# Gate and up projections of a two-block transformer kernel: the seven-product scheme applied inside each block product in every second weight slot

## The reference, cut to what matters

```python
def swiglu_ffn(u, w_gate_up, w_down):          # u (1, 512, 1024)
    g, up = jnp.split(u @ w_gate_up, 2, axis=-1)   # w_gate_up (1024, 2 * 2816)
    return (jax.nn.silu(g) * up) @ w_down          # w_down (2816, 1024)
...
D_MODEL, SEQ, DEPTH = 1024, 512, 2
D_FF = 2816
```

## Time and profile before

| | |
|---|---|
| median of 3 runs | 2923.05 us (2922.53 to 2923.17) |
| span of the profiled execution | 2921.3 us, first to last instruction |
| PE busy | 2810.8 us, 96% of the span |
| PE weight loads busy | 1896.7 us, 65% |
| DVE, ACT, POOL busy | 1110.9, 663.0, 512.2 us |
| gate and up, slots 1 to 10, layer 1 and layer 2 | about 242 us each, from 1674 and from 2538 us |

### The profile page before, as it was taken

One profiled execution on the slowest core, in us unless ns is written; L12 is line 12 of the kernel. 1 busy time (PEld: TensorE's weight loads), 2 busy tenths in 40 slices (PEclk: granted clock), 3 DMA queues, 4 the chain that ended last, 5 costly groups with the idle time before them and its releaser, 6 DMA issues.

```text
span 2921.3 us, 32166 instructions
## 1 busy us (share of the span) xinstructions
PE 2810.8 (96%) x12444; PEld 1896.7 (65%) x12444; DVE 1110.9 (38%) x2252; ACT 663.0 (23%) x1512; POOL 512.2 (18%) x785
## 2 busy tenths in 40 slices
PE   8999999899999998999999999999999999999998
PEld 4565543355656432686565688888686575788887
DVE  4543311154433111445432333354446332333354
ACT  3333110033331100105422211101206412211100
POOL 3101111131111111113200022201114410122201
PEclk9999999999999999999999999999999999999999
DMA  3206799831067998420020222222220111122222
GB/s 135 75 29 252 292 425 423 363 127 56 30 259 305 424 425 359 175 87 30 30 87 29 87 87 87 72 80 94 87 87 30 49 67 47 69 87 87 72 90 84
DMA packets 106579, 422.13 MB, mean 145 GB/s; under 512 B 10096, under 2 KB 14320, under 8 KB 91440
## 3 DMA queue, kind: packets, MB, share of 16 engines
q1 hardware_dynamic: 93104, 387.01, 34.1%
q0 software_dynamic: 12736, 30.84, 2.8%
q10 hardware_dynamic: 576, 2.10, 0.2%
HBM read 408.63 MB, written 27.26 MB: 149 GB/s over the span
## 4 chain that ended last, share of the span: by engine, by line
PE 77%; issue 9%; DMA 7%; DVE 2%; ACT 2%; POOL 1%; POOLq 1%; DVEq 0%; SPq 0%; ACTq 0%
PE ps L2551 35%; PE ps L1773 6%; DMA ring_feat<-in_w 5%; PE ps L431 5%; PE ps L2792 4%; PE ps L2819 4%; PE ps L1112 3%; PE ps L1814 3%; PE ps L2693 2%; PE ps L2839 2%; PE ps L3153 2%; PE ps L1339 2%; PE ps L2283 1%; PE ps L2070 1%; PE ps L2265 1%
## 5 line engine op out<-in xcount | busy, mean ns | idle before, releaser
L431 PE MATMUL ps<-ring_feat 128*128 128x512 f32 (+2 forms) x704 | 274.9, 545 | 4.9 <-DMA ring_feat<-in_w_lat 2.8
L2551 PE MATMUL ps<-ring_feat 128*128 128x256 f32 x1216 | 277.0, 379 | 1.6 <-ACT big L287 1.6
L2551 PE MATMUL ps<-big 128*128 128x256 f32 x1200 | 268.1, 379 | 0.0
L2551 PEld LDWEIGHTS ps<-ring_feat 128*128 128x128 f32 x1216 | 230.9, 190 | 34.5 <-issue 3.3
L2551 PEld LDWEIGHTS ps<-big 128*128 128x128 f32 x1200 | 228.0, 190 | 31.0
L431 PEld LDWEIGHTS ps<-ring_feat 128*128 128x128 f32 x704 | 132.7, 191 | 130.6 <-issue 93.6
L2551 PE MATMUL ps<-tmp 128*128 128x256 f32 x576 | 128.6, 379 | 0.0
L2551 PE MATMUL ps<-ring_feat,tmp 128*128 128x256 f32 x544 | 126.6, 379 | 0.0
L2551 PEld LDWEIGHTS ps<-tmp 128*128 128x128 f32 x576 | 109.3, 190 | 14.8
L2792 PE MATMUL ps<-ring_feat 128*128 128x512 f32 x256 | 113.9, 596 | 5.0 <-ACT ring_feat L3052 2.7
L1112 PE MATMUL ps<-ring_feat 128*128 128x512 f32 x256 | 113.7, 595 | 0.0
(11 more groups left out here) (501 smaller groups left out, 4663.8 us busy)
## 6 DMA issues: line engine op xcount, KB each, us to landing
big<-in_w SPq DMA_DIRECT2D x36, 2048.0 KB, 20.8
ring_feat<-in_w SPq DMA_DIRECT2D x36, 2048.0 KB, 27.7
ring_feat<-in_w_gate_up SPq DMA_DIRECT2D x22, 2048.0 KB, 8.0
ring_feat<-in_w_mix_in SPq DMA_DIRECT2D x12, 2048.0 KB, 8.1
e_spare<-in_w SPq DMA_DIRECT2D x12, 1792.0 KB, 25.7
par<-in_w SPq DMA_DIRECT2D x12, 1536.0 KB, 23.6
ring_feat<-in_w_down SPq DMA_DIRECT2D x12, 1536.0 KB, 6.7
tmp<-in_w_mem_kv SPq DMA_DIRECT2D x6, 2048.0 KB, 25.2
```

Of the source, the lines that this page charges most:

```text
L431: yield T.matmul(bank, lhs(k), rhs(k), start=k == 0, stop=k == n - 1)
L2551: m = T.matmul(to, lhs[:, j, :], rhs[:, j, :], start=start and j == 0, stop=stop and j == chunks - 1)
```

## The change

In slots 1 to 10 the two chunks of a slot are joined. Each of the seven products is now taken over the whole slot (256 columns of each half), in one order for all slots: P1, P6, P7, P5, P2, P4, P3. The intermediate `corner` blocks C11, C12, C21, C22 are four rows in SBUF. Two kinds of slot alternate:

- *One-level slots* (1, 3, 5, 7, 9), called O below: each product is two block products as before (8 matmuls of 128x128 against 256 tokens). The SBUF and PSUM operations around them are now 128x512, half as many.
- *Two-level slots* (2, 4, 6, 8, 10), `TWO_LEVEL`, called E below: each of the seven products is itself done by the seven-product scheme. Its operands are cut once more into 2x2 (two chunks by 128 columns, two chunks by 128 tokens), so a product is 7 x 2 = 14 matmuls of 128x128 against **128** tokens, and its result is 7 x 128 = 896 columns over two banks. The inner recombination is linear, so it is not done per product: the seven inner parts are carried through the outer additions, which become 128x896, and are recombined once per corner at the end (`corners`, POOL, seven additions of 128x256 for two corners at once).

For an E slot the inner sums of seven left operands have to be made (`form_left`, six by DVE with four operations of 128x256 each, and `weight_sums` for a22 by POOL), and once per layer those of the seven right operands (`form_right` two by DVE, `token_sums` five by POOL). They are kept in spare places (`spare_piece`) and in the parts of the slot that are no longer needed. The outer weight sums have one set of buffers, `s_block`, in place of two, so they are overwritten as soon as PE has used them. PSUM spaces are four, of two banks each, used in turn (`product_space`): a product waits until the one four before it has been read. The last multiplications of slot 10 (`gate_end`) move behind the down projection's second set of sums, and the down projection waits for them at its slot 3, not at slot 1.

The core of the diff:

```diff
+        X11, X12, X21, X22 = [(slice(k, k + 2), slice(f, f + P)) for f in (0, P) for k in (0, 2)]
+        SLOTS_UP = range(1, FC // 2)
+        TWO_LEVEL = range(2, FC // 2, 2)
+        PRODUCTS = ("P1", "P6", "P7", "P5", "P2", "P4", "P3")
+        LEFT = dict(P1="a11", P6="s2", P7="s3", P5="s1", P2="a12", P4="a22", P3="s4")
+        RIGHT = dict(P1="b11", P6="t2", P7="t3", P5="t1", P2="b21", P4="t4", P3="b22")
+        SEVEN = 7 * P
+        s_block = {f"s{i + 1}": view(big, 4096 + i * 1024, KC // 2, 256) for i in range(4)}
+        corner = view(big, 8192, 4, SEVEN)
...
+            def product(p, n):
+                w, to = slot_w["pe", n][1], product_space(l, p, n)
+                x, tok = left_block(w, LEFT[p]), RIGHT[p]
+                if n not in TWO_LEVEL:
+                    for i in range(2):
+                        m = block_product(to[:, i * 256:(i + 1) * 256], x[:, :, i * P:(i + 1) * P], right_block(tok))
+                    return m
+                y11, y12, y21, y22 = right_parts(tok)
+                s1, s2, s3, s4 = left_sums(l, w, LEFT[p])
+                t1, t2, t3, t4 = right_sums(l, tok)
+                for q, (lhs, rhs) in enumerate(((part(x, X11), y11), (part(x, X12), y21), (s4, y22), (part(x, X22), t4),
+                                                (s1, t1), (s2, t2), (s3, t3))):
+                    m = block_product(to[:, q * P:(q + 1) * P], lhs, rhs, 2)
+                return m
...
+            for n in SLOTS_UP:
+                two = n in TWO_LEVEL
+                for p in PRODUCTS:
+                    op, tok = LEFT[p], RIGHT[p]
+                    if p == "P1":
+                        ring_n = slot_w["pe", n][0]
+                        pe.wait_ge(w_loaded[ring_n % 2], 16 * (ring_n // 2 + 1))
+                    if two and op == "a22":
+                        pe.wait_ge(*outer(l, op, n))
+                    elif two or op[0] == "s":
+                        pe.wait_ge(*formed(l, op, n))
+                    if p == "P4":
+                        pe.wait_ge(*formed(l, "s4", n))
+                    if n == TWO_LEVEL[0] and tok in TOKENS_AT:
+                        pe.wait_ge(*tokens(l, tok))
+                    space_free(p, n)
+                    product(p, n).then_inc(bank_full if p == "P4" else up_full, 1)
...
+        def up_act(act, l):
...
+            for n in SLOTS_UP:
+                if n > 1:
+                    act.wait_ge(*added(l, "low", n - 1))
+                copy("P1", C11, n)
+                if n > 1:
+                    silu(C12, n - 1)
+                copy("P7", C21, n)
+                if n > 1:
+                    act.wait_ge(*added(l, "high", n - 1))
+                copy("P5", C22, n)
+                silu(C11, n)
+            silu(C12, LAST_UP)
...
+        def form_left(dve, l, op, n):
...
+            w = slot_w["dve", n][1]
+            x = left_block(w, op)
+            dve.drain()
+            form_sums(dve, *[part(x, b) for b in (X11, X12, X21, X22)], left_sums(l, w, op)).then_inc(blocks_summed, 1)
...
+        def up_dve(dve, l):
...
+            for n in SLOTS_UP:
+                two_now, two_next = n in TWO_LEVEL, n + 1 in TWO_LEVEL
+                if n > 1:
+                    last_corner(n - 1)
+                form_slot(dve, l, n)[3]()
+                if n > 1:
+                    multiply(0, n - 1)
+                if two_now:
+                    form_left(dve, l, "s4", n)
+                if n > 1:
+                    multiply(1, n - 1)
+                if n == 1:
+                    form_right(dve, l, "b11")
+                    form_right(dve, l, "t2")
+                dve.wait_ge(*full(l, "P6", n))
+                dve.wait_ge(*copied(l, "p1", n))
+                dve.drain()
+                V.tensor_tensor(corner[:, C12, 0:width_of(n)], product_space(l, "P6", n), corner[:, C11, 0:width_of(n)],
+                                ALU.add).then_inc(hidden_ready, 1)
+                if n < LAST_UP:
+                    third, second, first, fourth = form_slot(dve, l, n + 1)
+                    third()
+                    second()
+                    if two_next:
+                        dve.wait_ge(*full(l, "P1", n))
+                        form_left(dve, l, "a11", n + 1)
+                        form_left(dve, l, "s2", n + 1)
+                        form_left(dve, l, "s3", n + 1)
+                    first()
+                    if two_next:
+                        form_left(dve, l, "s1", n + 1)
+                else:
+                    dve.wait_ge(*full(l, "P7", n))
+                    down_sums(dve, l, 0, slot_w["dve", n][0] + 1)
+                add("P2", C11, n).then_inc(hidden_ready, 1)
+                dve.wait_ge(*outer(l, "c22", n))
+                add("P4", C21, n).then_inc(hidden_ready, 1)
+                if two_next:
+                    form_left(dve, l, "a12", n + 1)
+            last_corner(LAST_UP)
...
+        def up_pool(pool, l, before_end):
...
+            def corners(half, n):
+                pool.wait_ge(*added(l, ("c21", "c12")[half], n))
+                q = [in_halves[:, half, :, i * P:(i + 1) * P] for i in range(7)]
...
+                def add(to, more):
+                    return G.tensor_tensor(out=q[to], in0=q[to], in1=q[more], op=ALU.add)
...
+                add(5, 0)
+                add(1, 0)
+                pool.drain()
+                add(6, 5)
+                pool.drain()
+                add(5, 4)
+                add(3, 6)
+                pool.drain()
+                add(2, 5)
+                add(4, 6).then_inc(outer_added, 1)
...
+            for n in SLOTS_UP:
+                if n - 1 in TWO_LEVEL:
+                    corners(1, n - 1)
+                c12, c21, c22 = (corner[:, c, 0:width_of(n)] for c in (C12, C21, C22))
+                pool.wait_ge(*added(l, "u2", n))
+                pool.wait_ge(*copied(l, "p7", n))
+                G.tensor_tensor(out=c21, in0=c21, in1=c12, op=ALU.add).then_inc(outer_added, 1)
+                if n == 1:
+                    token_sums("t4")
+                pool.drain()
+                pool.wait_ge(*copied(l, "p5", n))
+                G.tensor_tensor(out=c12, in0=c12, in1=c22, op=ALU.add).then_inc(outer_added, 1)
+                pool.drain()
+                G.tensor_tensor(out=c22, in0=c22, in1=c21, op=ALU.add).then_inc(outer_added, 1)
+                if n + 1 in TWO_LEVEL:
+                    weight_sums(n + 1)
+                if n == 1:
+                    pool.wait_ge(bank_full, before_end)
+                    token_sums("t1")
+                    token_sums("b22")
+                if n in TWO_LEVEL:
+                    corners(0, n)
```

More of the change, by code:

```diff
@@ new lines, in program, with part, spare_piece @@
+        corner = view(big, 8192, 4, SEVEN)
+        C11, C12, C21, C22 = range(4)
+        in_halves = corner.rearrange("p (r h) n -> p h r n", h=2)
+        def part(v, block):
+            return v[:, block[0], block[1]]
+        def spare_piece(l, i):
+            for buf, first, n in ((e_spare, 0, 14), (rows, 0, 6), (cst, P, 14), (par[l], PAR2["mix_post"][0], 8),
+                                  (par[l], PAR2["sub_g"][0], 1), (big, 11776, 2)):
+                if i < n:
+                    return view(buf, first + i * 256, 2, P)
+                i -= n
@@ new lines, in up_act, with copy, silu @@
+        def up_act(act, l):
+            up_slots("act", l)
+            def copy(p, to, n):
+                act.wait_ge(*full(l, p, n))
+                A.activation(corner[:, to, 0:width_of(n)], product_space(l, p, n), ACT.Copy).then_inc(silu_ready, 1)
+            def silu(c, n):
+                if n in TWO_LEVEL:
+                    act.wait_ge(*outer(l, ("low", "high")[c], n))
+                else:
+                    act.wait_ge(*added(l, ("c11", "c12")[c], n))
+                gate = results(c, n)
+                A.activation(gate, gate, ACT.Silu).then_inc(silu_ready, 1)
+            for n in SLOTS_UP:
[10 more added lines that the diff above has]
+            silu(C12, LAST_UP)
@@ new lines, in gate_up @@
+            n = take(name, "ring")
+            w = ring_slot(n, KC, 512)
+            if name == "pe":
+                eng.wait_ge(w_loaded[n % 2], 16 * (n // 2 + 1))
+                first, second, banks = slice(0, 2 * P), slice(2 * P, 4 * P), []
+                feat_ready(eng, 1)
+                for i in range(2):
+                    for o, reader in ((i * P, "act"), (256 + i * P, "dve")):
+                        banks.append((open_bank(eng, reader), o))
+                        up_at[l, i] = count[("pe", "bank")] - 1
+                        products(banks[-1][0], w, o, first)
+                    if i == 0:
+                        turn_x(name, eng, TT - 1)
+                feat_ready(eng, 3)
+                for bank, o in banks:
+                    products(bank, w, o, second).then_inc(bank_full, 1)
+                    take(name, "full")
```

(19 more changed lines are left out.)

349 lines of the change are left out of this document (208 added, 141 removed).

## The result

The changed kernel takes 2939.63 us (median of four, 2935.82 to 2940.6) against 2922.89 for the kernel before (median of four; the 2923.05 above is that of three): a ratio of 1.0052 [1.0037, 1.0066], slower by half a per cent. I had forecast 2900.4 us, in a range of 2893 to 2917. PE's own work shrank about as forecast, but PE then waited for longer than it had saved.

What follows compares the result with a forecast made beforehand. PE, busy 96% of 2921.3 us and without a gap in this stage, was taken as the bound. Shorter E slots (-23.5) and stalls (+0.8) gave -22.7, so 2898.6, plus 1.75 from span to median: 2900.4 us, range 2893 to 2917.

Steps and rivals of the forecast that it cites:

- What bounds the kernel before, and PE's saving: Slots 1 to 10: PE's records set the time; E slots fall from 24.1 to 21.8 us, saving 23.5 in all.
- Rival 1: E slots: the pace of short records does not last over 196 in a row; no gain, 2923 us, chance 0.08.
- Single durations: DVE, ACT and POOL operations taken singly: for 128x896, DVE 1.09 us, ACT 0.9, POOL 2.1; POOL 1.27 for 512.
- At the ratio of rows 10 (+0.31 in 0.69) they cost DVE 1.2 to 1.7: O slot: POOL's three 512-wide additions delay DVE by 1.2 to 1.7 us, scaled from one DVE sum stretched beside POOL.
- 0.8 us for stalls of all kinds: Each of 8 transitions from O to the next E: 0.1 us of PE stall, 0.8 us in the sum.
- if they take turns wholly, 3.8: Same three POOL additions, dear end: DVE and POOL exclude each other, costing DVE 3.8 us and missing the slack by 0.6.
- The slack of 3.2 becomes 1.5 to 2.0: C11 of O, before P6 of the next E: 3.2 us early, still 1.5 to 2.0 after DVE's delays beside POOL.
- the heavy half: DVE's work after an E slot's second multiplication, through sums and additions to O's C11: from 33.5 to 45.8 us.
- The end of slot 10: Down projection's first sums come before C11 as now, `rest` due only at its slot 3; no cost set.
- Rival 2: Corners: POOL's additions slow to 1.53 us, PE stands 8 us in each of 8 transitions; 2964 us, chance 0.12.
- POOL's 20 token operations (15 us) lie under slots 0 and 1: Start of each layer: POOL's token sums, 15 us, are hidden under slots 0 and 1, costing PE nothing.

Runs made afterwards that it cites:

- e5: Changed kernel with POOL's three outer additions of every joined slot on 8 columns, not 512 or 896 (values wrong): 2901.37 us, 0.991 of the kernel before.
- e4: Changed kernel with POOL's fourteen corner additions on 2 x 8 elements, not 2 x 128 (values wrong): 2907.9 us, 0.9939 of the kernel before.
- e9: Changed kernel with the high half's seven corner additions moved from POOL to DVE: 2909.53 us, 0.9942 of the kernel before.
- e11: Changed kernel with POOL's outer and corner additions replaced by fills that read nothing (values wrong): 2903.61 us, 0.9923 of the kernel before.
- e7: Changed kernel with only slots 2, 5 and 8 two-level: 2914.3 us, 0.9956 of the kernel before.

## Why the prediction was wrong, step by step

- **What bounds the kernel before, and PE's saving: right.** An E slot takes 21.95 us against my 21.8, ten save 22.0 us against 23.5, and the pace of 0.112 holds for a slot of 196 records. Rival 1 fell. e5, where PE never waits in the stage, shows it whole: 46.04 us a pair.
- **Single durations: right where nothing meets.** POOL's 512 took 1.27 (forecast 1.27, the middle of a range of 1.09 to 1.45, so with some luck), DVE's 896 1.09 (1.09), ACT's 0.92 (0.9).
- **"At the ratio of rows 10 (+0.31 in 0.69) they cost DVE 1.2 to 1.7": this step failed.** Rows 10 hold no ratio. POOL's row ahead of those shown, from the trace of before:

```profile
1911.02 0.64 POOL L3140 TENSOR_TENSOR cst<-cst,rows 128x256 f32<-128x256 f32 x1 [9.59 <-ACT rows L3112]
```

It ends at 1911.66, and DVE's stretched sum (1911.20, 1.00) ends 0.54 us later. The DVE sum waited for the end of POOL's operation. It came out at +0.31 only because POOL's operation had 0.46 us left when it began. The earlier trace rows hold the full wait: POOL's 1.53 began 0.19 us into DVE's sum of 1.23 and ended 0.49 after it. I had written the price of full turns beside the sum and left it out for rows 10. The sum had 0.8 us for stalls of all kinds; PE's waits and the slow records behind them came to 17.0 + 17.4 = 34.4. The changed kernel shows the same at the end of slot 10, against POOL's 896-wide additions; DVE, then POOL, in order of time:

```profile
1905.57 2.57 DVE L2526 TENSOR_TENSOR big<-tmp 128x512 f32<-128x512 f32 x1
1908.21 2.42 DVE L2528 TENSOR_TENSOR big<-big,tmp 128x512 f32<-128x512 f32 x1
1910.70 2.41 DVE L2530 TENSOR_TENSOR big<-tmp,big 128x512 f32<-128x512 f32 x1
```

```profile
1905.13 2.46 POOL L3450 TENSOR_TENSOR big<-big 128x896 f32<-128x896 f32 x1 [7.02 <-DVE big L3369]
1907.75 2.33 POOL L3455 TENSOR_TENSOR big<-big 128x896 f32<-128x896 f32 x1 [0.16 <-issue]
1910.24 2.32 POOL L3457 TENSOR_TENSOR big<-big 128x896 f32<-128x896 f32 x1 [0.16 <-issue]
```

POOL's ends are 1907.59, 1910.08 and 1912.56; DVE's are 1908.14, 1910.63 and 1913.11, each 0.55 later. Three sums of 0.69 take 7.4 us. The stretched 1024-wide sums above end 1.1 us after the POOL operation that they met (1785.28 + 2.13 = 1787.41 against 1784.15 + 2.17 = 1786.32), the 256-wide ones 0.28 after it. A longer POOL operation makes a longer wait, and the change made them 3.5 times as wide. So the kind of price at the dear end of my range, "if they take turns wholly, 3.8", was right. That its size agrees with the 3.9 us measured over the pass is partly luck: POOL's three 512-wide additions cost DVE 2.9, and the other 1.0 came from POOL's sums of a22, which I had priced for POOL alone.

- **"The slack of 3.2 becomes 1.5 to 2.0": the wrong question even at the right price.** I laid out one pair from PE's beginning and held each operation against its deadline, one contact at a time. But C11 is late by what the corners before it were late by, and those by the u2 before them. Closed, the ring without turns is some 41.4 us, about what my own durations add up to, under PE's 46.1: a slack of 4.7 for all of it. Turns take 3.9 in the heavy half and beside a22, 2.5 at the 896-wide outer additions, which I had priced as if alone, and 0.5 at the corners: 2.2 us too many in each pass, and every pass adds its own. A slack that I put at 1.5 to 2.0 us was thus a lack of 2.2. With turns priced for the heavy half alone I got 0.6.
- **The end of slot 10 was not costed.** I wrote that the down projection's sums come before C11 "as now". They met POOL's additions there, and PE waited 3.5 us a layer.
- **A wait can cost PE its clock too.** Behind the waits 5.0 us in layer 1 and 3.5 in layer 2 went in records at half the clock, about 1.7 us for each of the five parts. This stood in no term of mine. Not every wait has one behind it: the 2.15 us wait of slot 8 has in layer 1 and has not in layer 2.
- **Rival 2, the side on which it came out, was right in its place and wrong in its mechanism.** It had PE idle before P6, for DVE, ACT's silu and POOL. But its condition was not met: the corner additions average 0.87 us, below the 1.17 from which it was to decide. The corners are a long part of the ring, and shortening them does help (e4, e9), but what made it too long was the turns between DVE's sums and POOL's additions (e11). I had only the large form of it (2964), so 2936 to 2941 lay between a rival and the range.
- **"POOL's 20 token operations (15 us) lie under slots 0 and 1": not quite.** The 0.8 us in slot 2, which every run with a two-level slot 2 has (0.6 to 1.5 us), save e5 and e11, stand before P5. In the list of PE, P5 of slot 2 waits for the token sums of t1. Their last operation on POOL, then PE:

```profile
1705.29 0.99 POOL L3408 TENSOR_TENSOR ring_feat<-big,rows 128x256 f32<-128x256 f32 x1
```

```profile
1706.38 1.58 PE L2545 MATMUL ps<-big 128*128 128x128 f32 x12 [0.63 <-issue]
```

PE goes on 0.10 us after POOL's end (1706.28), and e7 and e9 show the same 0.10 (1709.08 and 1709.18; 1706.86 and 1706.96). In e5 and e11 POOL is done by 1704.6 and 1703.3, before PE comes there. I had put this term at nothing.

Left open: the 3.5 to 4.8 us by which the other three executions were longer than the profiled one.

## What to carry to other kernels

Where work goes round between engines, add up the ring from one event to its own return and hold that against the bounding engine's period; an operation's slack against its deadline is spent once for the whole ring, not once for each contact. Where DVE's operation has two SBUF inputs and POOL's reads SBUF, charge each DVE operation that meets POOL the rest of POOL's operation and its own time, and keep POOL's operations there short. If a wait moves but the period stays when an operation is pulled forward, moving operations won't help: shorten the ring.

## What the runs showed of the hardware

- Two-input SBUF operations of DVE (512-wide, 0.69 alone) ended 0.54 to 0.55 us after the POOL operation that they met, in each of the four pairs shown, for POOL operations of 0.64 to 2.46 us. The 1024-wide sums took up to 3.10 in place of 1.23.
- DVE's addition of PSUM to SBUF kept its 1.08 us (128x896) beside a POOL addition of the same width.
- POOL fills of 128x896 (three in 2.77 us) left DVE's 1024-wide sums at 1.22 us.
- Short matmuls, each with a weight load of its own, keep 0.112 us a record over a slot of 196.
- Behind a wait of 4.1 us twelve of PE's records took 2.64 us in place of 1.50, in a stretch with a granted clock of 0.93.
